# One level of a seven-product scheme for the down projections of a two-block transformer kernel

## The reference

```
x = x + 0.5 * swiglu(rmsnorm(x, g_ffn1), w1_gate, w1_up, w1_down)      # FFN 1
h = rmsnorm(x, g_mix); p = h @ w_in; ... two attentions ...
x = x + concat([out_a, out_b]) @ w_out
x = x + 0.5 * swiglu(rmsnorm(x, g_ffn2), w2_gate, w2_up, w2_down)      # FFN 2
return rmsnorm(x, g_final)

def swiglu(x, w_gate, w_up, w_down):
    return (silu(x @ w_gate) * (x @ w_up)) @ w_down
```

## Time and profile before

| | |
|---|---|
| time, median of 3 runs | 2004.43 us (2004.12 to 2005.02) |
| profiled execution | span 2001.6 us; the page gives no time beside the span |
| TensorE busy | 1924.5 us, 96% of the span |
| DVE, ACT, Pool busy | 944.0, 548.6, 196.0 us |
| chain that ended last | PE 78%, SP's queue 8%, DVE 5%, DMA 4%, ACT 3% |
| granted TensorE clock, mean | 0.996 |
| down stage of FFN 1 | 1199.0 to 1320.5 us |

### The profile page before, as it was taken

The page is one execution under the profiler, slowest core; times in us unless marked ns, Lnnn a source line. Parts: engine busy times, 40 slices in busy tenths (PEclk is TensorE's granted clock), DMA queues, the critical chain, the costliest instruction groups (busy, mean ns, idle before and its releaser), DMA issues.

```text
span 2001.6 us, 24702 instructions
## 1 busy us (share of the span) xinstructions
PE 1924.5 (96%) x8909; PEld 1345.3 (67%) x8910; DVE 944.0 (47%) x1468; ACT 548.6 (27%) x840; POOL 196.0 (10%) x236
## 2 busy tenths in 40 slices
PE   8999999999997899997999999999999999999998
PEld 7888887884332233333788888886656688888886
DVE  4998983434111111113544443345796444444423
ACT  4234435341000000000522222233337642222222
POOL 2000000001111112111000000001237300000000
PEclk9999999999999999999999999999999999999999
DMA  6444232288999999999333322234110033333332
GB/s 206 151 138 126 85 100 90 84 365 315 425 425 426 427 426 395 421 426 373 94 96 101 97 94 95 93 98 108 60 54 5 12 95 95 94 94 107 102 96 74
DMA packets 153190, 358.70 MB, mean 179 GB/s; under 512 B 31756, under 2 KB 89537, under 8 KB 127898
## 3 DMA queue, kind: packets, MB, share of 16 engines
q1 hardware_dynamic: 147418, 349.64, 47.7%
q0 software_dynamic: 5680, 8.03, 1.1%
q10 hardware_dynamic: 16, 0.00, 0.0%
HBM read 348.29 MB, written 19.40 MB: 184 GB/s over the span
## 4 chain that ended last, share of the span: by engine, by line
PE 78%; SPq 8%; DVE 5%; DMA 4%; ACT 3%; issue 2%; POOL 1%; ACTq 0%; DVEq 0%
PE psum L508 15%; PE psum L510 15%; PE psum L509 15%; PE psum L1356 7%; SPq L1222 6%; PE psum L649 5%; PE psum L651 5%; PE psum L650 5%; PE psum L1366 3%; DMA expert_down_third<-in_w_expert_down_dram 2%; DMA arena<-in_w_expert_down_dram 2%; PE psum L2143 1%; PE psum L2176 1%; DVE arena L2498 1%; SPq L1225 1%
## 5 line engine op out<-in xcount | busy, mean ns | idle before, releaser
L503 DVE TENSOR_TENSOR w_lo<-w_raw,w_hi 128x1024 fp32r<-128x1024 f32 (+1 forms) x232 | 286.9, 1236 | 567.1 <-ACT w_hi L498 567.0
L508 PE MATMUL psum<-h_hi,w_hi 128*128 128x512 f32 x1240 | 488.1, 394 | 3.9 <-DVE h_lo L990 1.9
L510 PE MATMUL psum<-h_hi,w_lo 128*128 128x512 f32 x1240 | 483.4, 390 | 0.0
L509 PE MATMUL psum<-h_lo,w_hi 128*128 128x512 f32 x1240 | 483.1, 390 | 0.0
L498 ACT ACTIVATE w_hi<-w_raw 128x1024 fp32r<-128x1024 f32 (+1 forms) x232 | 245.1, 1056 | 862.1 <-PE psum L510 644.3
L508 PEld LDWEIGHTS psum<-h_hi,w_hi 128*128 128x128 f32 x1240 | 233.2, 188 | 56.7 <-issue 5.2
L509 PEld LDWEIGHTS psum<-h_lo,w_hi 128*128 128x128 f32 x1240 | 233.4, 188 | 49.4 <-issue 1.7
L510 PEld LDWEIGHTS psum<-h_hi,w_lo 128*128 128x128 f32 x1240 | 233.1, 188 | 48.8
L1356 PE MATMUL psum<-arena,w_raw 128*64 128x512 f32 x800 | 181.7, 596 | 13.4 <-DMA arena<-in_w_expert_up_dram 12.5
L1018 DVE SCALAR_TENSOR_TENSOR arena<-arena,vec 128x512 f32<-128x512 f32 x240 | 162.7, 752 | 1.0 <-ACT arena L845 1.0
L1491 ACT ACTIVATE w_raw<-psum 128x256 f32<-128x256 f32 x36 | 13.8, 383 | 461.7 <-PE psum L1356 461.7
(11 more groups left out here) (341 smaller groups left out, 2050.9 us busy)
## 6 DMA issues: line engine op xcount, KB each, us to landing
arena<-in_w_expert_gate_dram SPq DMA_DIRECT2D x44, 1024.0 KB, 23.3
arena<-in_w_expert_up_dram SPq DMA_DIRECT2D x44, 1024.0 KB, 26.2
arena<-in_w_expert_down_dram SPq DMA_DIRECT2D x22, 2048.0 KB, 28.9
w_raw<-in_w_in_dram SPq DMA_DIRECT2D x44, 512.0 KB, 3.7
w_raw<-in_w_gate_dram SPq DMA_DIRECT2D x88, 256.0 KB, 2.8
w_raw<-in_w_up_dram SPq DMA_DIRECT2D x88, 256.0 KB, 3.0
w_raw<-in_w_down_dram SPq DMA_DIRECT2D x44, 512.0 KB, 3.6
expert_down_third<-in_w_expert_down_dram SPq DMA_DIRECT2D x10, 2048.0 KB, 28.0
```

The source lines that it names most:

```text
L503: eng.tensor_tensor(wlo[:, s, :, 0:n], raw[:, slot, :, 0:n], whi[:, s, :, 0:n].bitcast(F32), ALU.subtract).then_inc(w_lo, 1)
L508: eng.matmul(o, w_h, x_h, start=first, stop=False)
L509: eng.matmul(o, w_h, x_l, start=False, stop=False)
L510: return eng.matmul(o, w_l, x_h, start=False, stop=last)
```

## The change

The product of each down stage, activations A (512 tokens x 2816) by weights B (2816 x 1024), is cut into quarters: tokens in two halves, inner tiles in even and odd ones, columns in two halves. It is then computed as seven products of quarters or of sums of quarters (`PRODUCTS`) instead of eight, each of 11 inner tiles x 2 token tiles x 3 matmuls, in that order, and added up with signs and a factor of one half. 

- Each product has five chunks of two inner tiles and one of one (`N_CH` = 6), so there are 42 chunks (`N_DN`) of 12 or 6 matmuls. Products 0, 2 and 6 use plain quarters of B, which SP loads into `raw` as before (`load_direct`). Products 1, 3, 4 and 5 use sums of quarters of B.
- These sums are built in one region of 11 tiles over `h_hi` and `h_lo`, which are free once the up stage is over. Pool issues the transfers: plain loads (`load_terms`) and accumulating loads (`add_terms`, `accum_op=ALU.add`), 36 in each FFN. An addition waits for the landing of the one before it on its chunk and for the last low part made of the old sum.
- Sums of activations (`s1`, `s2`, `s4`, and one in place) are made by Pool in the up stage, four operations of 128 x 256 behind each group (`token_sums`). The last group's four stand ahead of the transfers in Pool's program.
- `act` holds the activations in float32; the high and low parts of the stationary operand are now made for each chunk in the down stage (ACT `x_h`, DVE `x_l`, three slots `dxh`, `dxl`), with a third slot for the weights' parts too (`down_slots`). The two operations `products_hi` and `products_lo` of the up stage are gone.
- Joining the products adds on DVE and ACT: a copy of the first product (`kept`), six additions of two banks at once onto the residual rows, three additions of `kept`, and the last two row tiles one at a time (`last_rows`). Row tiles 2 and 3 are complete before 0 and 1; the next stage and the final norm take them in the order 2, 3, 0, 1.
- Some semaphores are merged so that new ones fit, and chunk counts behind the first down stage shift by 20.

```diff
+PRODUCTS = ("A11B11", "S3T3", "A12B21", "S2T2", "A22T4", "S1T1", "S4B22")
+FROM_DRAM = (0, 2, 6)
+N_CH = (N_UP + 1) // 2
+N_DN = len(PRODUCTS) * N_CH
+DSLOTS, TERMS = 3, 16 * 6
...
+        def down_weights(j):
+            return A[f"w{j + 1}_down_2"].rearrange("o (k e p) n -> p e (o k) n", e=2, p=P)
...
+        def operand_of(x):
+
+            prod, m = x // N_CH, x % N_CH
+            ks, first, second = slice(CK * m, CK * m + pair_size(m)), slice(0, HALF_T), slice(HALF_T, T)
+            return (act[:, ks, 0, first], act[:, ks, 0, second], act[:, ks, 1, first], s2[:, ks, :],
+                    act[:, ks, 1, second], s1[:, ks, :], s4[:, ks, :])[prod]
...
+            def load_direct(n):
+
+                m, x = n % N_CH, direct_at(n)
+                e, half = ((0, 0), (1, 0), (1, 1))[n // N_CH]
+                slot = (raw_of(C_DN[j]) + n) % RAW
+                sp.wait_ge(w_lo, C_DN[j] + (direct_at(n - RAW) if n >= RAW else n - RAW) + 1)
+                sp.dma_start(raw[:, slot, 0:pair_size(m), :], weight_quarter(down, m, e, half)).then_inc(w_raw[slot], 16)
...
-            for n in range(2 * N_UP):
-                half, kp = n // N_UP, n % N_UP
-                load_chunk(sp, C_DN[j] + n, (C_DN[j] + n) % RAW,
-                           down[:, 2 * kp:2 * kp + 2, half * CN:half * CN + CN])
...
+            def token_sums(g, i=0):
+
+                pool.wait_ge(evac[g % 2], seen(G_UP[j] + g) + i)
...
+                pool.tensor_tensor(a21, a11, a21, ALU.subtract).then_inc(sums_r, 1)
+                pool.wait_ge(sums_r, n + 1)
+                pool.tensor_tensor(s2[:, k, :], a22, a21, ALU.add).then_inc(sums_r, 1)
+                pool.wait_ge(sums_r, n + 2)
+                pool.tensor_tensor(s4[:, k, :], s2[:, k, :], a12, ALU.subtract).then_inc(sums_r, 1)
+                pool.tensor_tensor(s1[:, k, :], s2[:, k, :], a11, ALU.subtract).then_inc(sums_r, 1)
...
+            token_sums(N_UP - 1)
...
+            def add_terms(m, n, e, half):
+
+                terms_landed(pool, j, m, n)
+                pool.dma_start(summed(CK * m, pair_size(m)), weight_quarter(down, m, e, half), accum_op=ALU.add).then_inc(
+                    terms_in[m], 16)
+
+            def load_terms(m):
+                pool.dma_start(summed(CK * m, pair_size(m)), weight_quarter(down, m, 0, 1)).then_inc(terms_in[m], 16)
+
+            pool.wait_ge(w_used, C_DN[j])
+            for m in range(N_CH):
+                load_terms(m)
+            for m in range(N_CH):
+                add_terms(m, 1, 1, 1)
+            for m in range(N_CH):
+                pool.wait_ge(w_lo, C_DN[j] + N_CH + m + 1)
+                add_terms(m, 2, 0, 0)
+            for m in range(N_CH):
+                pool.wait_ge(w_lo, C_DN[j] + 3 * N_CH + m + 1)
+                add_terms(m, 3, 1, 0)
+            for m in range(N_CH):
+                pool.wait_ge(w_lo, C_DN[j] + 4 * N_CH + m + 1)
+                load_terms(m)
+            for m in range(N_CH):
+                add_terms(m, 5, 0, 0)
...
+            for x in range(N_DN):
+                prod, m = x // N_CH, x % N_CH
...
+                pe.wait_ge(w_lo, C_DN[j] + x + 1)
+                pe.wait_ge(dx_lo, N_DN * j + x + 1)
+                w_h, w_l, x_h, x_l = down_slots(x)
...
+                for a, t in order:
+                    f, o = slice(t * P, t * P + P), psum[:, banks[prod] + t, :]
+                    begin, end = m == 0 and a == 0, m == N_CH - 1 and a == n - 1
+                    pe.matmul(o, x_h[:, a, f], w_h[:, a, :], start=begin, stop=False)
+                    pe.matmul(o, x_l[:, a, f], w_h[:, a, :], start=False, stop=False)
+                    mm = pe.matmul(o, x_h[:, a, f], w_l[:, a, :], start=False, stop=end)
...
+            for x in range(N_DN):
+                prod, m = x // N_CH, x % N_CH
+                w_h, _, x_h, _ = down_slots(x)
...
+                    terms_landed(act, j, m, {1: 2, 3: 3, 4: 4, 5: 6}[prod])
+                act.wait_ge(w_used, C_DN[j] + (x - 1 if x < SPLIT else x - 2 if x >= DSLOTS else 0))
+                act.activation(w_h, weight_of(j, x), ACT.Copy).then_inc(w_hi, 1)
...
+                act.activation(x_h, operand_of(x), ACT.Copy).then_inc(dx_hi, 1)
+                if x == 2:
+                    gate(N_UP - 1)
...
-                products_hi(g - 1, i)
-                products_lo(g - 1, i)
...
+                if x == 2:
+                    products(N_UP - 1)
...
+                if x == 4 * N_CH + 2:
+                    dve.wait_ge(w_used, C_DN[j] + 4 * N_CH)
+                    dve.wait_ge(first_kept, j + 1)
+                    dve.scalar_tensor_tensor(out=kept, in0=psum[:, 2:4, :], scalar=-0.5, in1=kept, op0=ALU.mult,
+                                             op1=ALU.add).then_inc(joined, 1)
+                if x == 4 * N_CH + 3:
+                    join(both(2, 0))
+                if x == 4 * N_CH + 4:
+                    join(both(2, 1), ALU.subtract)
+                if x == 4 * N_CH + 5:
+                    join(both(0, 1), ALU.subtract)
...
+            for x in range(N_DN):
+                w_h, w_l, x_h, x_l = down_slots(x)
+                if x == 2:
+                    scaled(N_UP - 1)
+                dve.wait_ge(w_hi, C_DN[j] + x + 1)
+                dve.tensor_tensor(w_l, weight_of(j, x), w_h.bitcast(F32), ALU.subtract).then_inc(w_lo, 1)
+                dve.wait_ge(dx_hi, N_DN * j + x + 1)
+                dve.tensor_tensor(x_l, operand_of(x), x_h.bitcast(F32), ALU.subtract).then_inc(dx_lo, 1)
+                after(x)
```

More of the change, by code:

```diff
@@ L29 @@
 HALF = D // 2
+HALF_T = T // 2
 BIG = 1.0e5
@@ L1806, in sp_ffn @@
             load_group(N_UP - 1)
+            down = down_weights(j)
+            def load_direct(n):
[4 more added lines that the diff above has]
+                sp.dma_start(raw[:, slot, 0:pair_size(m), :], weight_quarter(down, m, e, half)).then_inc(w_raw[slot], 16)
+            for n in range(len(FROM_DRAM) * N_CH):
+                load_direct(n)
@@ new lines, in add_bank, with join, after @@
+            def add_bank(used, b, rows, scale=0.5):
+                dve.wait_ge(w_used, C_DN[j] + used)
+                return dve.scalar_tensor_tensor(out=rows, in0=psum[:, b:b + 2, :], scalar=scale, in1=rows, op0=ALU.mult,
+                                                op1=ALU.add)
+            def join(rows, op=ALU.add):
+                dve.wait_ge(joined, 8 * j + 5)
+                dve.tensor_tensor(rows, rows, kept, op).then_inc(joined, 1)
+            def after(x):
+                if x == 2:
+                    products(N_UP - 1)
+                if j == 0 and x == N_CH + 4:
+                    dve.wait_ge(rsq_r, 7 * TT)
+                if x == N_CH + 3:
+                    add_bank(N_CH, 4, both(0, 0)).then_inc(joined, 1)
+                if x == 2 * N_CH + 3:
+                    add_bank(2 * N_CH, 6, both(2, 1), -0.5).then_inc(joined, 1)
+                if x == 2 * N_CH + 4:
+                    add_bank(2 * N_CH, 6, both(2, 0)).then_inc(joined, 1)
+                if x == 3 * N_CH + 3:
+                    dve.wait_ge(joined, 8 * j + 1)
+                    add_bank(3 * N_CH, 0, both(0, 0)).then_inc(joined, 1)
+                if x == 4 * N_CH + 2:
[9 more added lines that the diff above has]
+                    join(both(0, 1), ALU.subtract)
+                if x == 5 * N_CH + 2:
+                    dve.wait_ge(joined, 8 * j + 6)
+                    add_bank(5 * N_CH, 4, both(2, 0)).then_inc(evac[G_DN[j] % 2], 1)
+                if x == 6 * N_CH + 1:
+                    mean_of_first(dve, 8 * TT if j == 0 else 12 * TT)
+                if x == 6 * N_CH + 2:
+                    dve.wait_ge(joined, 8 * j + 8)
+                    add_bank(6 * N_CH, 0, both(2, 1), -0.5).then_inc(x1_r, 1)
+                if x == 6 * N_CH + 3:
+                    dlink(dve, add_bank(6 * N_CH, 0, both(0, 1), -0.5))
+                if j == 0 and x == 6 * N_CH + 4:
+                    turned_low(dve, 5, 4, gain_of("g_mix_2"), range(4))
@@ new lines, in last_rows @@
+            def last_rows():
+                for t in range(2):
+                    if t == 0:
+                        dve.wait_ge(row_done, 2 * (TT - 1) * (j + 1) + j + 1)
+                    else:
+                        dve.wait_ge(w_used, C_DN[j] + N_DN)
+                    rows = rows_tok[:, t, HALF:D]
+                    dve.scalar_tensor_tensor(out=rows, in0=psum[:, 2 + t, :], scalar=-0.5, in1=rows, op0=ALU.mult,
+                                             op1=ALU.add).then_inc(evac[(G_DN[j] + 1) % 2] if t else x1_r, 1)
@@ L2674, in act_last @@
             act.activation(stat(V_OFF), stat(R_SUM), ACT.Sqrt)
-            for t in range(TT):
+            for n, t in enumerate(LAST_ROWS):
                 square_half(act, 3, 1, (t,))
```

332 lines of the change are left out of this document (191 added, 141 removed).

## The result

The kernel after takes 2032.76 us (median of 4 runs, 2030.47 to 2034.27), the kernel before on the same chip 2004.28 (4 runs): a ratio of 1.0144, 95% interval 1.013 to 1.0158. It is slower by 28.5 us. 2021 was forecast, in a range of 2002 to 2072: the sign and the mechanism hold, the loss is 12 us larger than booked.

What follows compares the result with a forecast made beforehand. TensorE was taken to bound both down stages. Per stage, -15.0 us of matmuls and +23.2 of waits and clock net +8.2; twice, +16.4 on 2001.6 gives 2018, plus 2.8 to the runs' median, 2021, range 2002 to 2072.

Steps and rivals of the forecast that it cites:

- matmuls taken away: Each down stage: 462 matmuls instead of 528 at an unchanged 0.2267 us, 15.0 us less per stage.
- start of product 0: First chunks of a down stage: TensorE waits 0.4, 0.3 and 1.5 us behind DVE's last-group work; product 0 ends 2.2 late.
- gap before product 1: TensorE idles 10.1 us for the first weight sum, behind Pool's token sums, six loads and the first addition.
- gap before product 5: TensorE idles 6.8 us because all six additions stand behind all six reloads in Pool's queue.
- clock: After both gaps TensorE runs at half clock for 3.3 us; each costs 1.8 us, 3.6 per stage.
- small: Small waits in products 3 and 4, whose additions are issued early; 0.5 us per stage.
- The rate of an addition: Accumulating 512 KB transfers on Pool's queue move twice the bytes, 2.5 us each.
- rival 1: Additions slower than TensorE eats: at 3.7 us each, 2043 us; at 5 us, 2091; chance 0.28.
- Rival 2: Gaps close: Pool issues in 0.37, additions land in 3.6; gaps 5.5 and 3.7, total 2000 or 1995 us; chance 0.11.
- Rival 3: ACT and DVE bind, not DMAs: Pool's reads slow DVE in product 4, +2 to +4 per stage, 2027 us; chance 0.07.

Runs made afterwards that it cites:

- Experiment 1: Against the kernel after, Pool issues the six plain loads of the first weight sum ahead of the last group's activation sums; 2020.90 us, ratio 1.0096.
- experiment 7: Kernel after with Pool's first loads ahead of the last activation sums and product 4's reloads interleaved with additions; 2012.15 us, ratio 1.005.
- Experiments 9 and 10: Kernel after with unread matmuls filling the gaps before products 1 and 5: 62 and 23 calls, 2054.70 us; then 31 and 12, 2027.20 us.
- experiment 5: Kernel after with SP issuing the sum region's plain loads and Pool's first six additions ahead of its last token sum; 1999.89 us, ratio 0.998.
- Experiments 8 and 11: Kernel with SP's region loads: A12B21 made second, S3T3 third, 2006.81 us; or product 2's direct loads held until product 1's fourth chunk is split, 2005.64 us.

## Why the prediction was right, and where it was off

Its terms for a down stage, in us; measured from the starts of the matmuls of FFN 1 and 2:

| term | booked | FFN 1 | FFN 2 |
|---|---|---|---|
| matmuls taken away | -15.0 | -15.0 | -15.0 |
| start of product 0 | +2.2 | +2.7 | +2.8 |
| gap before product 1 | +10.1 | +15.0 | +15.0 |
| gap before product 5 | +6.8 | +6.1 | +6.4 |
| clock | +3.6 | +5.6 | +4.3 |
| small | +0.5 | +1.1 | +0.2 |
| sum | +8.2 | +15.5 | +13.7 |

(The small term of FFN 1 is the wait of 0.74 for the first chunk of the mixer and a rest of 0.4.) Together 29.2 of the span's 29.7; behind the last matmul the program takes 0.5 longer, where 0 was booked.

**The matmuls** are exact: 66 x 8 against 66 x 7 at 0.2267, and nowhere else does TensorE gain.

**The start of product 0** is right: waits of 0.45 and 1.65 where 0.4, 0.3 and 1.5 were booked, and `products` ready at t = 8.4, as forecast. Each wait costs some 0.2 us beyond its length, since the first matmul behind it is slower to be followed.

**The gap before product 1 is the step that failed, in its size.** Booked were sums until t = 11.5, the first addition issued at 17.8 and landed at 24.2, product 1 at 27.2. Measured: 14.1, 20.0, 29.8 and 32.8. The difference of 5.6 is made of four parts. The sums took 5.6 us and not 3.1 (+2.6 with the wait before them): I had 0.75 for each, but all four start while a subtraction of DVE is running, and take 1.64, 1.06, 1.60 and 1.18 for 0.74. The issue of six loads took 4.3 for the 6.3 booked (-2.0): a direct DMA from Pool costs 0.72, less than a gather in the earlier trace rows. But then the first addition had to wait 1.6 for the landing of the first load, which I had not booked at all. And it took 9.8 us until ACT had its result, where 6.4 were booked (+3.4): between 1216 and 1223 the queues still moved plain loads at a DMA share over 1.0. Experiment 1 takes these parts away and gains 8.0 of the 14.8. Product 0's own end came 0.7 late, so the gap grew by 4.9. I had given the queue 0.4 us to drain; it had six region loads in it.

**The rate of an addition,** the largest unknown, was right: twice the bytes, 2.5 us booked, 2.53 measured, and rival 1 (3.7 us and more) did not occur. In the second gap, with a nearly empty queue, the first addition of product 5 took 6.1 us from issue to ACT, against 5.95. So that gap was well placed: 6.1 and 6.4 for 6.8. The Trainium skill's figure for a GpSimd DMA ("DMA: Bandwidth & Descriptors", section "Anatomy of one DMA — SWDGE (gpsimd) path"), 3.2 us for 512 KB, is below the shortest plain load of that size in the kernel after, which landed 4.1 us after the start of its issue (3.3 after its end), and far below an addition (5.7 at the least); had I gone by it, the forecast would have been further off.

**The clock** was put 2.0 (FFN 1) and 0.7 too low. The gap's length is not what decides it: behind 14.8 us of idling 14 and 10 matmuls ran at 0.43, behind 5.9 and 6.2 it was 13 and 10, behind 6.8 in experiment 1 nine, behind 7.7 in experiment 7 six. So a gap costs 1.3 to 2.9 us of clock, and 1.8 was one value out of that spread. Experiments 9 and 10 show that this excess is clock. A long gap isn't needed either: behind a wait of 2.53 us (experiment 5, FFN 2, product 5) eight matmuls were slow and cost 1.5 us.

**The rivals.** Rival 2, the gaps close, would have needed a quick Pool. Its issue was quick for a plain load (0.72) but not for an addition (1.20), and the landing was not. The 5.5 us that rival 2 has for the first gap don't come out of its own terms: 11.5 + 6 x 0.37 + 3.6 + 0.4 + 3.0 - 17.1 is 3.6, which puts that rival at about 1996 and not 2000. Nothing in the main sum hangs on it. Rival 3 did not show: products 3 and 4 run at 14.96. The mutual slowdown of Pool and DVE, which I had used for rival 3 only, acted in the first gap instead. The Trainium skill has this as a rule ("SBUF — State Buffer", section "Who interferes with whom"): a DVE operation with two SBUF inputs and a GpSimd operation that reads SBUF hold each other up. This trace agrees. Of Pool's 88 sums of activations, the 28 that start while such a subtraction is running take 1.06 to 1.72 us, and the 60 others 0.73 to 0.74; DVE's 128x512 subtraction goes from 0.68 to 1.22. The up stage shows it too, where in 16 of 20 groups the third sum (L1911) is the one caught:

```profile
1036.33 0.74 POOL L1909 TENSOR_TENSOR token_sums<-products  x1 [0.21 <-POOL products L1907]
1036.77 1.39 DVE L528 TENSOR_TENSOR w_lo<-w_raw,w_hi 128x1024 fp32r<-128x1024 f32 x1 [1.69 <-ACT w_hi L523]
1037.27 1.48 POOL L1911 TENSOR_TENSOR token_sums<-token_sums,products  x1 [0.19 <-POOL token_sums L1909]
1038.72 0.73 POOL L1912 TENSOR_TENSOR token_sums<-token_sums,products  x1
```

**What the cause is made of.** The saving of 29.9 us is there, and is given back in waits for transfers. Order on Pool's queue costs 19 us (experiment 7). Moving the plain loads to SP, with Pool's first additions ahead of its last sums, gives another 12 to 14 (experiment 5, 2000 for 2012 us and 0.998 for 1.005). What then stays, some 25 us against a TensorE-bound run of 1974, lies by the starts of the matmuls in products 0 and 1 (15.8 in the two FFNs) and around the reload (products 4 and 5, 10.1). Experiments 8 and 11 moved the first part to other products and made it 6 to 7 us larger. In both, transfers that were needed later ran beside those needed first. Whether the two queues, ordered by need, would win these 25 us, or the DMA engines' load keeps them, stays open. How much would be left with weight sums in another place, or made by an idle engine, was not tried.

## What to carry to other kernels

Where transfers feed the bound engine, draw up two timetables before taking work off it: one of the queue that issues them, instruction by instruction with all its waits, and one of bytes by rate, in which an accumulating transfer counts twice. Then ask of every stretch which transfers run side by side, and whether those of one queue are needed later than those of the other: beside additions, direct loads landed 4.0 us apart, where TensorE uses up a chunk in 2.72. The first addition of a chain pays every step of both timetables: the sums ahead, the loads' issue, the first landing, the backlog and its own latency. A saving on the bound engine shortens the time in which the transfers have to arrive, so a share of 0.3 before says little about the share in the stretch that follows the change.

## What the runs showed of the hardware

- An accumulating transfer of 512 KB from DRAM passes every 2.53 us at 205 GB/s with a DMA share of 1.1, where plain ones reach 410 to 427. Pool issues it in 1.20 us (plain 0.72) and it lands 5.7 us after the start of its issue at the least, a plain one 4.1.
- Where additions of Pool's queue and plain loads of SP's, 512 KB each, run side by side, each kind lands 4.0 us apart, at 262 GB/s together (experiments 8 and 11).
- Pool and DVE slow each other on elementwise work in SBUF: a Pool sum of 128x256 takes 0.73 to 0.74 us, and 1.06 to 1.72 when it starts while DVE subtracts; DVE's 128x512 subtraction goes from 0.68 to 1.22.
- After a wait the lower clock lasts for 6 to 14 matmuls of 512 columns, with no relation to the wait's length between 6 and 15 us. It also fell behind idle stretches of 2.02 (experiment 10), 2.27 (11), 2.53 (5) and 3.11 us (8), with work already going on again, and not behind 1.53 and 2.20 (10).
- A float32 matmul call of 256 columns (the filling of experiments 9 and 10) leaves two records and takes 0.433 us.
